# Column sums of the adaLN modulation rows: four TensorE transposes and a VectorE sum in place of four one-column products

## The chip, the cores and the metric

The kernel runs on one core of a Trainium2 chip. The metric is the device time of one execution in microseconds. A core has a matrix engine (TensorE, PE in the rows; its weight loads are listed apart as PEld), a vector engine (VectorE, DVE), a scalar engine (ScalarE, ACT), GpSimd (POOL) and a queue engine (SyncE, SP) that here issues the transfers from device memory. Products land in PSUM, in banks of 128 partitions by 512 fp32 columns.

## The reference

Two decoder layers over 256 tokens of width 1024. Each layer takes six vectors of 1024 numbers (shift, scale and gate for each of two halves) from the conditioning vector `c`:

```python
for l in range(DEPTH):
    mod = jax.nn.silu(c) @ ada_w[l] + ada_b[l]                 # (1, 6144)
    sh1, sc1, g1, sh2, sc2, g2 = jnp.split(mod[:, None, :], 6, axis=-1)
    h = rms_norm(x, norm_mix[l]) * (1.0 + sc1) + sh1
    x = x + g1 * token_mixing(h, ...)                          # three attention-like mixers, gates, w_out
    h = rms_norm(x, norm_ffn[l]) * (1.0 + sc2) + sh2
    f = swiglu(h, ...) if l % 2 == 0 else moe_ffn(h, ...)      # dense, then top-2 of 8 experts
    x = x + g2 * f
return rms_norm(x, final_norm)
```

All weights are fp32. `mod` is computed from `c` and `ada_w` alone, 2 x 6144 sums of 1024 products.

## The kernel before, in words

**Weights.** SP loads each weight as chunks of 1 MB (128 x 2048 fp32) into six buffers `raw`. ScalarE rounds a chunk to `w_hi` (line 1435) and VectorE computes the rest `w_lo` (line 1852), so that TensorE can build an fp32 product from three products of rounded parts (`mm3`, lines 743 to 745). In the first 970 us of the profile this goes in halves of a chunk with four slots (`HL`), and the engines split three halves ahead of TensorE (`AHEAD`). The expert stage after that uses whole chunks (`wide_hi`, `wide_lo`).

**Order.** The order of the work is written out by hand. The token-mixing stage of each layer follows the string `SLOTS`: before each piece of a large product stand the small steps of the mixers, among them `d` (a pair of modulation products) and `s` (its column sum); `KEPT` says which of them a layer keeps, six in layer 0 and four in layer 1. In the dense stage of layer 0 the class `Due` says after which chunks a pair and a sum come. Every engine runs through the same list, so each engine has its own queue in that order.

**Modulation.** The 12288 columns come in 24 blocks of 512. For a block, `ada_pair` multiplies the two chunks of `ada_w` (kept in fp32) with `silu(c)`. The 1024 rows are eight groups of 128; group k of a chunk goes to the quarter k of the partitions (32 partitions that all hold the same number), so a 128 x 512 bank `pO` then holds four partial rows, each 32 times. ScalarE copies it to the tile `acc` (`ada_copy`). Then the partial rows must be added and turned so that 512 columns become 128 partitions by 4 numbers of `mod`. Two functions do this: `ada_sum` writes a bank of `pT` and serves the `s` steps and the dense stage; `ada_sum_early` writes a bank of `pO` and serves the places around the norms. In both, four products use a 128 x 128 piece of `acc` as the stationary operand and the tile `quads` as the moving one. `quads` is one column that is 1 in the first partition of each quarter and 0 elsewhere, made once by VectorE from the identity matrix (line 2210).

VectorE then adds the bias and writes `mod` (`ada_columns`, line 1868, and `ada_columns_early`, line 1875). `mod` is used by `modulate` (line 1996 writes `hf`, the modulated rows), by `gate_row` (which spreads a gate over a bank) and, for the experts, at line 2426.

**Transposes.** Other parts of the kernel turn 128 x 128 fp32 blocks with TensorE transposes against the identity, four to a bank of `pT`, in the helper `turned` (line 801). Small products go through the helper `mm` (line 748).

**Waits.** `link` lets VectorE wait for the completion of its own last instruction before the next one issues. `take_T` and `take_O` make TensorE wait until the bank used two takes ago has been read; `free` is the semaphore that says so.

The functions that the diff touches and what calls them, with the line numbers of the profile:

Of the kernel before, what the change touches and what calls it, by code (L numbers as in the profile page):

```python
# [27 lines left out]
ALU = mybir.AluOpType  # L28
# [3 lines left out]
P = 128  # L32
# [313 lines left out]
def build(nc, a, table, out):  # L346
    ctx = ExitStack()
    with ctx:
        def sem(name):
            return ctx.enter_context(nc.semaphore(name))  # L350
# [41 lines left out]
        rope_t = sb("rope_t", [P, 8, HD])  # L392
        tmp = sb("tmp", [P, W])

        quads = sb("quads", [P, 1])
        acc = sb("acc", [P, W], at=(here[0] + 31) // 32 * 32)
        oT_hi[0] = sb("oTn_hi", [P, 4, SEQ], F32R)
        oT_lo[0] = sb("oTn_lo", [P, 4, SEQ], F32R)
# [105 lines left out]
        cols_ready = sem("cols_ready")  # L504
        csilu_ready = sem("csilu_ready")
        ada_used = sem("ada_used")
        quads_ready = sem("quads_ready")
        dve_link = sem("dve_link")
        act_link = sem("act_link")
        pool_link = sem("pool_link")  # L510
# [211 lines left out]
        def _(pe):  # L722
# [24 lines left out]
            def mm(dst, lhsT, rhs, first=True, last=True):  # L747
                return nc.tensor.matmul(dst, lhsT, rhs, start=first, stop=last, skip_group_check=True)  # L748
# [107 lines left out]
            def ada_sum():  # L856

                pe.wait_ge(O_free[b.O.slot(partials[0])], b.O.before(partials[0]) + 1)
                pt = take_T()
                for k in range(4):  # L860
                    ins = mm(pt[:, k:k + 1], acc[:, k * P:(k + 1) * P], quads[:, 0:1])
                ins.then_inc(T_full, 1)

            def ada_sum_early():

                pe.wait_ge(O_free[b.O.slot(partials[0])], b.O.before(partials[0]) + 1)
                po = take_O()
                for k in range(4):
                    ins = mm(po[:, k:k + 1], acc[:, k * P:(k + 1) * P], quads[:, 0:1])
                ins.then_inc(O_full, 1)  # L870

            pe.wait_ge(csilu_ready, 1)
            pe.wait_ge(quads_ready, 1)
            for j in range(EARLY):
                for _ in range(2):
                    b.adas.append(b.raw.take())
# [955 lines left out]
        def _(dve):  # L1832
# [24 lines left out]
            def ada_ended(first):  # L1857

                for what, n in due.after(first, b.hl.n // 2):
                    if what == "pair":  # L1860
                        skip(b.O, 1)
                    else:
                        ada_columns(n // ADA, n % ADA * 4, 1)

            def ada_columns(l, at, n):

                pt, free = T_in()
                V.tensor_tensor(mod[:, l, bass.ds(at, 4 * n)], pt[:, 0:4 * n], cols[:, l, bass.ds(at + R_ADAB, 4 * n)], ALU.add).then_inc(free, 1)

            def ada_columns_early(n):  # L1870

                l, at = n // ADA, n % ADA * 4
                skip(b.O, 1)
                po, free = O_in()
                V.tensor_tensor(mod[:, l, at:at + 4], po[:, 0:4], cols[:, l, at + R_ADAB:at + R_ADAB + 4], ALU.add).then_inc(free, 1)

            def ada_scale(l, at, w, n=8):

# [328 lines left out]
            link(V.memset(sq[:, :, :], 0.0))  # L2207
            dve.wait_ge(tab_in, 16)
            dve.wait_ge(cols_ready, DEPTH)
            V.tensor_reduce(quads[:, :], ident.rearrange("p (k n) -> p k n", k=CK)[:, :, 0], AX_X, ALU.add).then_inc(quads_ready, 1)  # L2210
            dve.wait_ge(x_in, 16)
            skip(b.raw, 2 * EARLY)
            for l in range(DEPTH):
# [31 lines left out]
                for subs, kind, which, i in MIXES[l]:  # L2245
                    for sub, c in subs:
                        if sub in ("k0", "kw", "kl", "k2", "k3"):
                            compression(sub, l)
                        elif sub in ("f0", "f1"):
                            forget_gates(sub, l)  # L2250
                        elif sub in ("a2", "a3"):
                            scores(sub, c, l)
                        elif sub[0] == "b" and o_uses(sub, c):
                            values(sub, c, l)
                        elif sub in ("a1", "a1b", "b1", "b2"):
                            skip(b.T, t_uses(sub, c))
                        elif sub == "o":
                            for q in range(2):
                                pt, free = T_in()
                                dve.wait_ge(oT_hi_ready, 6 * l + 2 * c + q + 1)  # L2260
                                V.tensor_tensor(oT_lo[c][:, 2 * q:2 * q + 2, :], pt[:, :].rearrange("p (k n) -> p k n", k=2),
                                                oT_hi[c][:, 2 * q:2 * q + 2, :].bitcast(F32), ALU.subtract).then_inc(oT_ready, 1)
                                dve.drain().then_inc(free, 1)
                        elif sub == "d":
                            skip(b.O, 1)
                        elif sub == "m":
                            lo_merged(0, 2)
                        elif sub == "s":
                            ada_columns(n_pair // ADA, n_pair % ADA * 4, 1)
                            n_pair += 1  # L2270
                    if last:
                        ended(*last, l)
                        if last == ("r", (2, 0), 1):
                            dve.drain().then_inc(merged_ready, 1)
                    split_to(b.hl.n + 1 + AHEAD)
                    b.hl.take()
                    last = (kind, which, i)
# [330 lines left out]
```

## Time and profile before

| | us |
|---|---|
| median of three runs | 2006.43 |
| lowest, highest | 2006.08, 2016.94 |
| profiled execution, first to last instruction (span) | 2005.2 |
| TensorE busy in it | 1933.1 (96%) |
| VectorE busy | 1473.8 (73%) |
| ScalarE busy | 1157.9 (58%) |

For the profiled execution only the span is listed; its own time is the span and about 1.2 us around it, if it lies as the median of the runs does (2006.43 - 2005.2). Busy time of TensorE has to be read with care: its matmuls overlap, the duration of one reaches into the next, and the distance from the start of one to the start of the next says what it costs. A matmul of fp32 operands is recorded twice (two passes), a transpose once.

```profile
PE   5999999999999999998999999999999999999996
PEclk9999999999999999999899999999999999999998
DMA  9745434585556644354799999999999999999993
```

These three lines cut the span into 40 slices of 50 us and give tenths: busy TensorE, the clock that it was granted, and the busy share of the 16 DMA engines. The modulation work lies in the first 20 slices, the experts in the other 20.

### The profile page before, as it was taken

The numbers are of one execution on the slowest core, as the hardware profiler recorded it, in microseconds if no ns is written. First come the engines' busy times: TensorE is split into PE (matmuls) and PEld (weight loads), VectorE is DVE, ScalarE is ACT, GpSimd is POOL, SyncE is SP. The second block draws the span as 40 slices with busy tenths as digits, with TensorE's granted clock in tenths as the row PEclk, the third lists the DMA queues.
The fourth block names the chain that finished last, engine by engine and source line by source line (L and its number), as shares of the span: only waits on it lengthen the run. The fifth ranks groups of instructions, "written<-read, shape, count | busy, mean of one in ns | idle before, by whom it ended". The sixth has DMA issues, their size and how long they took to land.

```text
span 2005.2 us, 27891 instructions
## 1 busy us (share of the span) xinstructions
PE 1933.1 (96%) x9976; PEld 1572.7 (78%) x9976; DVE 1473.8 (73%) x1504; ACT 1157.9 (58%) x1245; POOL 92.4 (5%) x134
## 2 busy tenths in 40 slices
PE   5999999999999999998999999999999999999996
PEld 2777888789987788887787787887878878778885
DVE  2755575744566655666788888889888888888988
ACT  1554554334434545543567767767677676766773
POOL 0510100000004300000000000000000000000000
PEclk9999999999999999999899999999999999999998
DMA  9745434585556644354799999999999999999993
GB/s 325 254 168 209 170 126 168 189 315 189 189 188 211 222 155 152 106 174 141 273 358 335 340 345 356 343 343 343 337 354 351 336 341 351 348 352 330 351 359 134
DMA packets 275630, 532.97 MB, mean 266 GB/s; under 512 B 10768, under 2 KB 23392, under 8 KB 275424
## 3 DMA queue, kind: packets, MB, share of 16 engines
q1 hardware_dynamic: 275552, 531.91, 75.6%
q8 instruction: 52, 0.85, 0.2%
q14 instruction: 26, 0.21, 0.0%
HBM read 530.83 MB, written 1.05 MB: 265 GB/s over the span
## 4 chain that ended last, share of the span: by engine, by line
PE 90%; DVE 5%; ACT 2%; issue 1%; DVEq 1%; DMA 0%; SPq 0%; ACTq 0%
PE pA L743 18%; PE pA L744 17%; PE pA L745 17%; PE pA L748 9%; PE pO L748 7%; PE pO L743 6%; PE pO L745 6%; PE pO L744 6%; PE pT L801 4%; DVE w_lo L1852 1%; PE pT L748 1%; ACT w_hi L1435 1%; DVE win L2085 0%; DMA x<-in_x 0%; PE pT L743 0%
## 5 line engine op out<-in xcount | busy, mean ns | idle before, releaser
L1893 DVE TENSOR_TENSOR wide_lo<-raw,wide_hi 128x2048 fp32r<-128x2048 f32 x336 | 762.5, 2290 | 123.2 <-ACT wide_hi L1435 103.6
L1435 ACT ACTIVATE wide_hi<-raw 128x2048 fp32r<-128x2048 f32 x336 | 644.7, 1921 | 214.6 <-PE pO L745 119.9
L1435 ACT ACTIVATE w_hi<-raw 128x1024 fp32r<-128x1024 f32 (+1 forms) x242 | 251.3, 1045 | 341.2 <-PE pA L745 249.8
L1852 DVE TENSOR_TENSOR w_lo<-raw,w_hi 128x1024 fp32r<-128x1024 f32 (+1 forms) x242 | 294.5, 1230 | 168.7 <-ACT w_hi L1435 159.7
L743 PE MATMUL pA<-wide_hi,x_lo 128*128 128x512 f32 x896 | 359.7, 401 | 1.4 <-DVE x_lo L2435 0.6
L745 PE MATMUL pA<-wide_hi,x_hi 128*128 128x512 f32 x896 | 355.0, 396 | 0.0
L744 PE MATMUL pA<-wide_lo,x_hi 128*128 128x512 f32 x896 | 354.9, 396 | 0.0
L743 PE MATMUL pA<-w_hi,h_lo 128*128 128x512 f32 (+2 forms) x560 | 227.4, 406 | 14.8 <-DVE w_lo L1852 10.9
L745 PE MATMUL pA<-w_hi,h_hi 128*128 128x512 f32 (+2 forms) x560 | 217.9, 389 | 0.0
L744 PE MATMUL pA<-w_lo,h_hi 128*128 128x512 f32 (+2 forms) x560 | 217.8, 389 | 0.0
L743 PEld LDWEIGHTS pA<-wide_hi,x_lo 128*128 128x128 f32 x896 | 168.7, 188 | 44.4 <-issue 3.8
L745 PEld LDWEIGHTS pA<-wide_hi,x_hi 128*128 128x128 f32 x896 | 168.5, 188 | 40.5
L744 PEld LDWEIGHTS pA<-wide_lo,x_hi 128*128 128x128 f32 x896 | 168.7, 188 | 38.1
L743 PE MATMUL pO<-wide_hi,aT_lo 128*128 128x512 f32 x448 | 180.1, 402 | 1.2 <-DVE aT_lo L2450 1.2
L745 PE MATMUL pO<-wide_hi,aT_hi 128*128 128x512 f32 x448 | 177.2, 396 | 0.0
L744 PE MATMUL pO<-wide_lo,aT_hi 128*128 128x512 f32 x448 | 176.9, 395 | 0.0
L743 PEld LDWEIGHTS pA<-w_hi,h_lo 128*128 128x128 f32 x560 | 107.7, 192 | 49.9 <-issue 22.3
L745 PEld LDWEIGHTS pA<-w_hi,h_hi 128*128 128x128 f32 x560 | 107.5, 192 | 23.2
L744 PEld LDWEIGHTS pA<-w_lo,h_hi 128*128 128x128 f32 x560 | 107.8, 193 | 19.3
L743 PEld LDWEIGHTS pO<-wide_hi,aT_lo 128*128 128x128 f32 x448 | 84.1, 188 | 21.7 <-issue 1.5
L745 PEld LDWEIGHTS pO<-wide_hi,aT_hi 128*128 128x128 f32 x448 | 84.2, 188 | 20.5
L744 PEld LDWEIGHTS pO<-wide_lo,aT_hi 128*128 128x128 f32 x448 | 84.3, 188 | 20.0
(273 smaller groups left out, 2391.1 us busy)
## 6 DMA issues: line engine op xcount, KB each, us to landing
raw<-in_moe_w SPq DMA_DIRECT2D x336, 1024.0 KB, 6.8
raw<-in_w_in SPq DMA_DIRECT2D x56, 1024.0 KB, 5.5
raw<-in_ada_w SPq DMA_DIRECT2D x48, 1024.0 KB, 6.6
raw<-in_ffn_w SPq DMA_DIRECT2D x33, 1024.0 KB, 5.2
raw<-in_w_out SPq DMA_DIRECT2D x8, 1024.0 KB, 5.0
raw<-in_cmp_k_w SPq DMA_DIRECT2D x4, 1024.0 KB, 5.9
raw<-in_cmp_v_w SPq DMA_DIRECT2D x4, 1024.0 KB, 10.6
raw<-in_w_read_nsa SPq DMA_DIRECT2D x4, 1024.0 KB, 6.1
```

Source lines behind the costliest of these rows:

```text
L743: nc.tensor.matmul(dst, xl, wh, start=first, stop=False, skip_group_check=True)
L744: nc.tensor.matmul(dst, xh, wl, start=False, stop=False, skip_group_check=True)
L745: return nc.tensor.matmul(dst, xh, wh, start=False, stop=last, skip_group_check=True)
L748: return nc.tensor.matmul(dst, lhsT, rhs, start=first, stop=last, skip_group_check=True)
L801: ins = nc.tensor.transpose(pt[0:m, i * width:i * width + n], src, ident[0:n, 0:n])
L1435: return nc.scalar.activation(dst, src, ACT.Copy)
L1852: V.tensor_tensor(w_lo[m][:, 0:n], raw[s][:, i * n:(i + 1) * n], w_hi[m][:, 0:n].bitcast(F32), ALU.subtract).then_inc(raw_done, 1)
L1893: V.tensor_tensor(wide_lo[m][:, :], raw[g][:, :], wide_hi[m][:, :].bitcast(F32), ALU.subtract).then_inc(raw_done, 2)
```

## The change

The four products with `quads` become four transposes of the same 128 x 128 pieces of `acc`, each into its own 128 columns of the bank. The column p of a transposed piece holds partition p of `acc`, so the four partial rows stand in columns 0, 32, 64 and 96 of each piece. VectorE sums them: one reduction reads 4 x 4 elements per partition, 32 columns apart, from PSUM and writes 4 numbers to `mod`; it waits for its own result (`link`), adds the bias in place and only then frees the bank. `quads`, its semaphore and the wait for it are gone, and the tiles allocated behind it move down by 32 bytes.

```diff
-        quads = sb("quads", [P, 1])
...
-                    ins = mm(pt[:, k:k + 1], acc[:, k * P:(k + 1) * P], quads[:, 0:1])
+                    ins = nc.tensor.transpose(pt[:, k * P:(k + 1) * P], acc[:, k * P:(k + 1) * P], ident)
                 ins.then_inc(T_full, 1)
...
-                    ins = mm(po[:, k:k + 1], acc[:, k * P:(k + 1) * P], quads[:, 0:1])
+                    ins = nc.tensor.transpose(po[:, k * P:(k + 1) * P], acc[:, k * P:(k + 1) * P], ident)
                 ins.then_inc(O_full, 1)
...
-            pe.wait_ge(quads_ready, 1)
...
+            def column_sums(l, at, pt, free):
+
+                link(V.tensor_reduce(mod[:, l, at:at + 4], pt[:, :].rearrange("p (j q n) -> p j q n", j=4, q=CK)[:, :, :, 0], AX_X, ALU.add))
+                V.tensor_tensor(mod[:, l, at:at + 4], mod[:, l, at:at + 4], cols[:, l, at + R_ADAB:at + R_ADAB + 4], ALU.add).then_inc(free, 1)
+
+            def ada_columns(n):
 
                 pt, free = T_in()
-                V.tensor_tensor(mod[:, l, bass.ds(at, 4 * n)], pt[:, 0:4 * n], cols[:, l, bass.ds(at + R_ADAB, 4 * n)], ALU.add).then_inc(free, 1)
+                column_sums(n // ADA, n % ADA * 4, pt, free)
 
             def ada_columns_early(n):
 
-                l, at = n // ADA, n % ADA * 4
                 skip(b.O, 1)
                 po, free = O_in()
-                V.tensor_tensor(mod[:, l, at:at + 4], po[:, 0:4], cols[:, l, at + R_ADAB:at + R_ADAB + 4], ALU.add).then_inc(free, 1)
+                column_sums(n // ADA, n % ADA * 4, po, free)
...
-            V.tensor_reduce(quads[:, :], ident.rearrange("p (k n) -> p k n", k=CK)[:, :, 0], AX_X, ALU.add).then_inc(quads_ready, 1)
```

## Rows read from the trace of the kernel before

**Rows 1.** Busy time by stretch: us, engines with counts, PEclk, DMA share, GB/s.

```profile
11.00:970.00 959.00, 915.62 (x5399) 753.31 (x5400) 569.69 (x841) 435.86 (x692) 91.96 (x129) 0.97 0.57 194
970.00:1985.00 1015.00, 1012.97 (x4565) 816.82 (x4566) 888.20 (x634) 716.74 (x547) 0.00 (x0) 1.00 0.95 340
```

**Rows 2.** Waits of TensorE from 0 to 985 us: total us, times, longest.

```profile
PE pA L743 <- DVE w_lo L1852: 11.9, 7, 4.6
...
PE pO L748 <- ACT acc L1435: 4.1, 1, 4.1
```

**Rows 3.** The one-column products: duration ns min/median/max, first and last start, forms.

```profile
L748 PE MATMUL pT<-quads,acc x112: 164/250/271, 68.7 to 781.2; 128*128 128x1 f32 x112
...
L748 PE MATMUL pO<-quads,acc x80: 169/250/375, 19.7 to 958.3; 128*128 128x1 f32 x80
```

**Rows 4.** Timeline of TensorE, one group between large products: start us, us, instruction.

```profile
68.69 0.95 PE L748 MATMUL pT<-quads,acc 128*128 128x1 f32 x8
69.50 0.48 PE L743 MATMUL pA<-w_hi,h_lo 128*128 128x512 f32 x1
```

**Rows 5.** Timeline of TensorE, four existing transposes between large products.

```profile
295.37 0.60 PE L801 MATMUL pT<-tab,S 128*128 128x128 f32 x4
295.72 0.48 PE L743 MATMUL pA<-w_hi,oTr_lo 128*128 128x512 f32 x1
```

**Rows 6.** Timeline of TensorE at the half clock, transposes and then a group.

```profile
598.30 1.97 PE L801 MATMUL pT<-tab,y 128*128 128x128 f32 x8 [2.98 <-DVE y L1986]
...
600.06 1.71 PE L748 MATMUL pO<-quads,acc 128*128 128x1 f32 x8
...
601.70 3.50 PE L748 MATMUL pO<-raw,csilu 128*32 128x512 f32 x16
```

**Rows 7.** Timeline of VectorE, a linked reduction out of PSUM and its successor.

```profile
957.78 0.17 DVE L2401 TENSOR_REDUCE rs<-pA 128x1 f32<-128x8 f32 x1 [1.38 <-PE pA L748]
957.98 0.17 DVE L2402 TENSOR_TENSOR rs<-pA,rs 128x16 f32<-128x16 f32 x1
```

**Rows 8.** Groups by line and shape, VectorE: busy us, mean ns, idle before.

```profile
L2045 DVE TENSOR_REDUCE stat<-S 128x8 f32<-128x120 f32 x4 | 1.1, 278 | 0.1
```

**Rows 9.** Waits of VectorE from 0 to 985 us.

```profile
DVE w_lo L1852 <- ACT w_hi L1435: 159.7, 102, 6.0
```

**Rows 10.** Timeline, TensorE group or transposes and the VectorE instruction that reads them.

```profile
25.83 0.95 PE L748 MATMUL pO<-quads,acc 128*128 128x1 f32 x8
...
26.82 0.16 DVE L1875 TENSOR_TENSOR mod<-pO,cols 128x4 f32<-128x4 f32 x1 [5.04 <-PE pO L748]
...
392.45 0.60 PE L801 MATMUL pT<-tab,y 128*128 128x128 f32 x4
...
393.09 0.99 DVE L1996 TENSOR_SCALAR hf<-pT,mod 128x256 f32<-128x256 f32 x2 [0.63 <-PE pT L801]
```

**Rows 11.** Timeline, the last sum of the dense stage.

```profile
437.42 1.05 PE L748 MATMUL pT<-quads,acc 128*128 128x1 f32 x8 [0.72 <-ACT acc L1435]
...
437.92 0.69 DVE L2330 TENSOR_TENSOR aTd_lo<-a_T,aTd_hi 128x512 fp32r<-128x512 f32 x1 [2.27 <-ACT aTd_hi L1435]
438.52 0.15 DVE L1868 TENSOR_TENSOR mod<-pT,cols 128x4 f32<-128x4 f32 x1
```

**Rows 12.** Timeline of TensorE, the waits behind the last two sums.

```profile
944.35 1.85 PE L748 MATMUL pA<-routw,hf 128*128 128x8 f32 x8 [1.53 <-DVE hf L1996]
...
960.80 6.66 PE L748 MATMUL pA<-sel,y 128*128 128x128 f32 x32 [2.24 <-DVE mod L1875]
```

**Rows 13.** Busy time by stretch, columns as in rows 1: clock at three places.

```profile
741.50:744.90 3.40, 3.40 (x9) 2.65 (x8) 2.69 (x7) 0.00 (x0) 0.00 (x0) 0.50 0.46 175
180.00:186.00 6.00, 6.00 (x36) 4.78 (x33) 4.97 (x7) 3.65 (x11) 0.00 (x0) 1.00 0.02 7
...
216.80:217.60 0.80, 0.80 (x9) 0.78 (x8) 0.00 (x0) 0.52 (x1) 0.00 (x0) 1.00 1.06 402
```

**Rows 14.** Groups by line and shape, TensorE transposes: busy us, mean ns, idle before.

```profile
L801 PE MATMUL pT<-tab,S 128*128 128x128 f32 x144 | 20.1, 275 | 0.0
```

More of the change, by code:

```diff
@@ L506, in build @@
         ada_used = sem("ada_used")
-        quads_ready = sem("quads_ready")
         dve_link = sem("dve_link")
@@ L1862, in ada_ended @@
                     else:
-                        ada_columns(n // ADA, n % ADA * 4, 1)
-            def ada_columns(l, at, n):
+                        ada_columns(n)
+            def column_sums(l, at, pt, free):
+                link(V.tensor_reduce(mod[:, l, at:at + 4], pt[:, :].rearrange("p (j q n) -> p j q n", j=4, q=CK)[:, :, :, 0], AX_X, ALU.add))
+                V.tensor_tensor(mod[:, l, at:at + 4], mod[:, l, at:at + 4], cols[:, l, at + R_ADAB:at + R_ADAB + 4], ALU.add).then_inc(free, 1)
+            def ada_columns(n):
                 pt, free = T_in()
-                V.tensor_tensor(mod[:, l, bass.ds(at, 4 * n)], pt[:, 0:4 * n], cols[:, l, bass.ds(at + R_ADAB, 4 * n)], ALU.add).then_inc(free, 1)
+                column_sums(n // ADA, n % ADA * 4, pt, free)
             def ada_columns_early(n):
-                l, at = n // ADA, n % ADA * 4
                 skip(b.O, 1)
                 po, free = O_in()
-                V.tensor_tensor(mod[:, l, at:at + 4], po[:, 0:4], cols[:, l, at + R_ADAB:at + R_ADAB + 4], ALU.add).then_inc(free, 1)
+                column_sums(n // ADA, n % ADA * 4, po, free)
             def ada_scale(l, at, w, n=8):
@@ L2268, in _ @@
                         elif sub == "s":
-                            ada_columns(n_pair // ADA, n_pair % ADA * 4, 1)
+                            ada_columns(n_pair)
                             n_pair += 1
```

## The prediction

> **What bounds the kernel now.** I read the busy time by stretch first. Between 11 and 970 us, where all modulation work lies, TensorE is busy for 915.62 of 959 us while VectorE is busy for 569.69, ScalarE for 435.86, and the DMA share is 0.57; after 970 us it is busy for 1012.97 of 1015 us [rows 1]. So TensorE bounds both parts, and the second part has none of the changed work: it only starts earlier or later. Next come the waits of TensorE in the first part. They are few and short, the largest sum being 11.9 us for `w_lo`, and on the changed path the largest is 4.1 us, for the copy to `acc` ahead of the first sum [rows 2]. What the reader is to see: outside such waits, a microsecond taken off TensorE's queue is a microsecond off the end, and one added to VectorE mostly is not.
>
> **How many.** The one-column matmuls are recorded 112 times into `pT` and 80 times into `pO` [rows 3]. A sum has four of them, each recorded twice, so there are 192 / 8 = 24 sums, 14 and 10.
>
> **TensorE, per sum.** Durations mislead here, since they overlap: start-to-start distances count. A group of one-column products between two large products takes 69.50 - 68.69 = 0.81 us [rows 4]. Four existing fp32 transposes in the same surroundings take 295.72 - 295.37 = 0.35 us [rows 5]; the product behind shows the same 0.48 us in both, so nothing is hidden in it. The old group costs four matmuls in two passes with a weight load each, the transpose one pass. The saving is 0.46 us; I take 0.45, because at some places a group is followed by something other than a large product.
>
> The Trainium skill, TensorE: Matmul & The Clock Gate, in its section on why a gap is 56 ns, puts the start-to-start floor of a tiny matmul near 25 ns and that of 128 columns at 55.6 ns. By it alone eight one-column passes (0.20 us) would cost no more than four transposes (0.22 us), and the sum of this document would be nought. The row shows 0.81 us, four times that, so the matmul floor is not what paces the group here.
>
> **Where it counts.** Of the 24 sums, 19 stand in TensorE's queue with other TensorE work right behind them and no wait that ends elsewhere: 19 x 0.45 = 8.55 us. The other five:
> - At 25.83 us, and in the same form once more behind the same norm, the sum heads a chain through `mod`, `hf` and the first split to a TensorE wait. What counts is the time to VectorE's next instruction: 26.82 - 25.83 = 0.99 us before; four transposes are read after 393.09 - 392.45 = 0.64 us [rows 10]. The gain of 0.35 us less the VectorE term below (0.20) is 0.15 us each, 0.3 together.
> - At 437.42 us `mod` is held by VectorE's `aTd_lo`, which starts at 437.92, takes 0.69 us and comes from ScalarE, not by the sum [rows 11]: no gain, and VectorE's 0.20 us is added.
> - Behind the last sum but one TensorE waits 1.53 us for `hf` [rows 12], which VectorE makes ahead of this `mod`: no gain, no loss.
> - Behind the last one it waits 2.24 us until VectorE has read the bank [rows 12]. VectorE comes to it late, after the router's chain, so nothing is gained and 0.20 us is added.
>
> **The half clock.** At 600.06 us the clock is low, and the group takes 601.70 - 600.06 = 1.64 us against (600.06 - 598.30) / 2 = 0.88 us for four transposes [rows 6]. That would save 0.76 us, but what follows then runs at the low clock for longer; I keep 0.45 and leave the rest to the range. The first sum is alike.
>
> **VectorE, per sum.** Added is one reduction (16 elements read from PSUM, 4 written) with a wait for itself. The nearest row is a linked reduction of 8 elements out of PSUM: its successor starts 957.98 - 957.78 = 0.20 us after it [rows 7]. That is the lower bound too. The upper bound is the reduction of 120 elements, 0.278 us [rows 8], with the 0.03 us that the wait leaves in rows 7 between end and start: 0.31. I take 0.20, since rows 7 have the same form and nearly the size. In all 24 x 0.20 = 4.8 us of VectorE. Queued behind it are mostly the next `w_lo` subtraction or `hf`. VectorE itself waits 159.7 us, 102 times, for ScalarE's `w_hi` in this part [rows 9], and the splits run three halves ahead, so this cover absorbs it; without the cover all 4.8 us would come back. Where the halves restart behind a norm (once in the dense stage of layer 0, once in the mixing of layer 1; both are among the seven waits for `w_lo` or their like in rows 2) VectorE's chain may be tight; I charge 0.1 us each, half a reduction.
>
> **Banks.** A bank of `pT` or `pO` is freed 0.20 us later after a read that starts up to 0.35 us earlier. Nil. ScalarE's copy, SP's queue and the transfers are unchanged: no DMA is added or moved, and the buffers of `ada_w` are released by `ada_pair`, not by the sum. POOL is not touched. The removed wait for `quads` and its one reduction lie in front of TensorE's first load of `ada_w`, which ends later: nil. The tiles move by 32 bytes: nil.
>
> **Sum.** -8.55 - 0.3 + 0.2 + 0.2 + 0.2 = -8.25 us. Against the profiled execution this is 2005.2 - 8.25 = 1996.95 us of span; the median of the runs stands 1.2 us above the span, so I predict 1998.2 us, 0.4% less.
>
> **Rival 1: nothing is left of it.** Either the transpose of `acc` paces like the products did (for instance because it is recorded in two passes after all, which would be the change not doing what it says), or the shorter queue turns into waits for `w_lo`. Against it: four transposes of this shape have four records [rows 5]. For it: every late VectorE term counted would return 4.8 us. Time: 2006.43 - 8.25 + 4.8 = 2003.0 if only VectorE's time returns, 2006.4 if the pace is as before, 2011 with both. Chance 0.14.
>
> **Rival 2: slower, by the clock.** The clock is granted for stretches of time, and the same token-mixing sequence ran at 1.00 in layer 0 (180 to 186 us) but at 0.50, the 1.2 GHz level, for 3.4 us in layer 1 (741.5 to 744.9 us) [rows 13]. Such a stretch costs at most half of itself, 1.7 us. Transposes in place of products, in the ten sums that `KEPT` leaves to the mixing stages and the nine others inside dense stretches, might let the clock fall behind each of them. The gain of 8.25 us is used up at five added stretches; with one behind each of the 19 it is 19 x 1.7 - 8.25 = +24.1, 2030.5 us. Against it: eight transposes in a row at 216.8 us ran at 1.00 with 1.00 behind [rows 13]. Chance 0.05, of which 0.03 beyond 1%.
> The Trainium skill, same page, section on PE-mode transpose, says that the full clock "doesn't engage for transpose-mode". By that rule this rival would be the rule and not the exception. The row at 216.8 us does not agree with it.
>
> **Rival 3: by the durations.** If the recorded durations were the cost, a sum would fall from 8 x 0.25 = 2.0 us [rows 3] to 4 x 0.275 = 1.1 us [rows 14]: 24 x 0.9 = 21.6 us, 1984.8 us. Against it: the start-to-start distances of the groups above. Chance 0.02.
>
> **How the numbers follow.** The forecast has 0.79. Its own range: down to 24 x 0.46 + 2 x 0.3 for the low-clock sums + 1.7 x 2 if two of the low stretches go, 2006.43 - 15 = 1991.4; up to the gain with VectorE at 0.31 on ten of its sums and one added stretch, 2006.43 - 8.25 + 3.1 + 1.7 = 2003. The range 1992 to 2006 adds the greater part of rival 1. A measurement of this kernel can tell a change of about 1% from none, and the whole gain is 0.4%: faster by over 1% is below 1986.4 us, which only rival 3 reaches; slower by over 1% is above 2026.5, which only rival 2 reaches.
>
> **What would show it.** In the profile after: 24 x 4 transposes of `acc` at one record each; 0.35 us from the start of a group to the next product (at 0.8 the first step is wrong); `mod` reductions near 0.17 us with the sum behind them 0.20 us later; TensorE's wait for `w_lo` in total no more than 1 us above 11.9; the wait before the gather near 2.24 + 0.45 + 0.20 = 2.9 us; the expert stage starting about 8 us earlier and of the same length. A clock below 0.97 in the first part would speak for rival 2. The prediction is wrong if the end moves by less than 3 us although the groups shrink as said.

## The result and the profile after

| | us, median of 6 | lowest to highest | profiled span |
|---|---|---|---|
| before | 2006.51 | 2006.04 to 2019.20 | 2005.2 |
| after | 1995.86 | 1995.13 to 1997.09 | 1993.3 |

The ratio is 0.9923, with a 95% interval from 0.9897 to 0.9950. The change takes 10.65 us off; forecast were 8.25, to 1998.2 us. Direction and order of size came out as said, and the time lies in the range. The forecast itself lies just outside the interval, whose smallest gain is 10.0 us. (The ratio also counts the two runs of the kernel before that took 2016.94 and 2019.20 us, so it shows more than the medians do.) The run that was profiled took 1995.13 us, 1.8 us above its span and not 1.2, which doesn't touch the gain. So something worth about 2.4 us was missing, and the experiments look for it.

Busy time by stretch of the kernel after, the columns as in rows 1:

```profile
11.00:960.00 949.00, 903.64 (x5304) 737.59 (x5305) 573.67 (x866) 436.18 (x692) 92.05 (x129) 0.98 0.57 196
960.00:1975.00 1015.00, 1011.32 (x4567) 814.76 (x4565) 889.64 (x635) 717.42 (x550) 0.00 (x0) 1.00 0.95 340
```

Against [rows 1] TensorE is still busy for nearly all of both parts (95% and 99.6%). The first part has shrunk by ten microseconds, the second is as it was; the first expert product starts at 959.47 us instead of 969.82. All but 1.6 of the 11.9 us between the two profiled spans were won ahead of the experts.

The transposes of `acc` by tile, kernel after (duration in ns min/median/max, first and last start in us):

```profile
L859 PE MATMUL pT<-tab,acc x56: 271/273/328, 68.0 to 773.7; 128*128 128x128 f32 x56
...
L867 PE MATMUL pO<-tab,acc x40: 272/273/473, 20.1 to 947.9; 128*128 128x128 f32 x40
```

56 + 40 = 96 = 24 x 4: one record each, where [rows 3] had eight records for a sum. Timeline of TensorE, kernel after, at the place of [rows 4]:

```profile
67.98 0.60 PE L859 MATMUL pT<-tab,acc 128*128 128x128 f32 x4
68.33 0.48 PE L741 MATMUL pA<-w_hi,h_lo 128*128 128x512 f32 x1
```

From group to product it is 0.35 us instead of 0.81, as the existing transposes had shown [rows 5]. VectorE at the same place:

```profile
68.62 0.17 DVE L1864 TENSOR_REDUCE mod<-pT 128x4 f32<-128x16 f32 x1 [0.92 <-PE pT L859]
68.83 0.16 DVE L1865 TENSOR_TENSOR mod<-mod,cols 128x4 f32<-128x4 f32 x1
```

The reduction takes 0.17 us and the sum starts 0.21 us behind it, as [rows 7]. Waits of TensorE and then of VectorE, kernel after, from 0 to 985 us (in total, times, longest), against [rows 2, 9]:

```profile
PE pA L741 <- DVE w_lo L1849: 12.2, 8, 4.8
...
PE pO L867 <- ACT acc L1432: 4.2, 1, 4.2
...
PE pA L746 <- DVE mod L1865: 2.3, 1, 2.3
...
PE pT L746 <- DVE mod L1865: 1.5, 1, 1.5
```

```profile
DVE w_lo L1849 <- ACT w_hi L1432: 160.0, 101, 6.8
```

TensorE waits 0.3 us more for `w_lo` in all: VectorE's added 5 us are absorbed. The wait for `mod` ahead of the gather is 2.3 us, where 2.9 had been forecast. The one for `hf` ahead of the router's first product has grown from 1.53 to 1.88 us: from the group to that product it is 2.48 us in both kernels, so nothing is won there, as forecast.

One more view, the clock. Timeline of TensorE, kernel after, at the place of [rows 6], and behind it three stretches of the same kernel, the columns as in rows 1. The first two hold the work that the kernel before does about 5.6 and 7.5 us later, from 741.5 and 813 us on:

```profile
595.15 1.97 PE L799 MATMUL pT<-tab,y 128*128 128x128 f32 x8 [3.01 <-DVE y L1987]
596.91 1.06 PE L867 MATMUL pO<-tab,acc 128*128 128x128 f32 x4
597.90 3.55 PE L746 MATMUL pO<-raw,csilu 128*32 128x512 f32 x16
```

```profile
735.90:739.30 3.40, 3.40 (x19) 2.80 (x18) 2.73 (x8) 0.62 (x1) 0.00 (x0) 1.00 0.39 148
805.40:809.40 4.00, 4.00 (x19) 3.31 (x18) 3.90 (x6) 1.51 (x3) 0.00 (x0) 1.00 0.00 0
...
181.70:188.50 6.80, 6.80 (x21) 5.23 (x20) 3.11 (x9) 0.83 (x1) 0.00 (x0) 0.52 0.00 0
```

At the low clock the group behind the norm at the start of layer 1 takes 0.99 us instead of 1.64. The work that ran at 0.50 from 741.5 us [rows 13] runs at 1.00 now, and so does that of the stretch at 813 us, which before stood at 0.57 (its row is below). In exchange 6.8 us from 181.7 us are at 0.52, and the same work (185.5 to 192.3 us there) stood at 1.00 before. The low stretches have moved, and they have become fewer.

What stands ahead of the two stretches is of use later. Timeline of TensorE, first the kernel before at 739 us, then the kernel after at the same work:

```profile
739.23 1.99 PE L748 MATMUL pO<-vc,PT 15*128 15x64 f32 x16
741.15 0.56 PE L743 MATMUL pA<-w_hi,h_lo 128*128 128x512 f32 x1
```

```profile
733.67 1.99 PE L746 MATMUL pO<-vc,PT 15*128 15x64 f32 x16
735.59 0.50 PE L741 MATMUL pA<-w_hi,h_lo 128*128 128x512 f32 x1
```

The change touches neither instruction. Small products of the mixers stand right ahead of the low stretch, and the nearest one-column group of the kernel before starts at 728.67 us, 12 us earlier. The low stretch at 181.7 us of the kernel after stands behind the same products in layer 0.

**A measure for the clock.** Every run comes with its span and its mean granted clock. The granted level is 1.00 or 0.50 of 2.4 GHz, so 2 x (1 - mean clock) x span is the time spent at the low level; I call it low-clock time. Over all runs of this study, taken within each kernel, the span grows by 0.44 us with each us of it (a least-squares slope over 193 runs). This gives a second number per kernel, the corrected span = mean span - 0.44 x low-clock time, in which instructions and waits are left and the clock is not. It is an estimate worked out from the runs. Its standard error is at most 1 us for each kernel (single runs scatter by 0.7 to 2.3 us), and the mean clock is listed to 0.001, so the low-clock time of one run comes in steps of 4 us. The kernel before has runs near 2018 us among its usual 2007 (22 of 80 over the whole study), with 89.3 us of low-clock time against 66.6, which is why means and medians differ here, and why a comparison with its mean and one with its usual runs give two numbers.

### The profile page after: what moved, and what is told of

It reads as the page before. It is cut to its first block, busy times and chain, and to the rows that moved or that the text cites. A ratio compares the mean times of both kernels' runs of the same rounds, so it can differ in the third digit from the quotient of the medians.

```text
span 1993.3 us, 27723 instructions
## 1 busy us (share of the span) xinstructions
PE 1919.3 (96%) x9880; PEld 1555.2 (78%) x9880; DVE 1476.8 (74%) x1527; ACT 1157.7 (58%) x1245; POOL 92.5 (5%) x134
## 3 DMA queue, kind: packets, MB, share of 16 engines
HBM read 530.83 MB, written 1.05 MB: 267 GB/s over the span
## 4 chain that ended last, share of the span: by engine, by line
PE 89%; DVE 6%; ACT 2%; issue 1%; DMA 1%; DVEq 1%; SPq 0%; ACTq 0%
PE pA L741 18%; PE pA L743 17%; PE pA L742 17%; PE pA L746 8%; PE pO L746 7%; PE pO L741 6%; PE pO L743 6%; PE pO L742 6%; PE pT L799 4%; DVE w_lo L1849 1%; ACT w_hi L1432 1%; DMA raw<-in_ffn_w 1%; PE pT L746 0%; DMA x<-in_x 0%; DVE win L2086 0%
## 5 line engine op out<-in xcount | busy, mean ns | idle before, releaser
L746 PE MATMUL pA<-h_hi,w_lo 128*128 128x256 f32 x352 | 99.0, 281 | 0.6 <-DVE w_lo L1849 0.6
```

## The experiments

All kernels in one table; "products" counts the groups of one-column products in each, and a set is a group of four transposes of `acc`.

| kernel | runs | median us | products | low-clock us | corrected span |
|---|---|---|---|---|---|
| before | 80 | 2007.2 | 24 | 72.9 | 1976.0 |
| after | 6 | 1995.9 | 0 | 59.8 | 1967.8 |
| e1_pe_twice (24 sets more) | 10 | 2005.6 | 0 | 59.3 | 1976.2 |
| e2_dve_twice | 9 | 1996.8 | 0 | 60.3 | 1969.6 |
| e3_before_shift1 | 10 | 2007.6 | 24 | 63.0 | 1978.0 |
| e4_before_shift2 | 10 | 2010.2 | 24 | 69.1 | 1979.3 |
| e5_after_shift1 | 10 | 1995.5 | 0 | 55.8 | 1969.8 |
| e6_after_shift2 | 10 | 1999.2 | 0 | 60.7 | 1971.0 |
| e7_before_twice | 4 | 2044.9 | 48 | 105.2 | 1995.7 |
| e8_late_only | 10 | 2002.8 | 10 | 68.9 | 1971.2 |
| e9_pe_three (48 sets more) | 10 | 2012.2 | 0 | 56.7 | 1985.6 |
| e10_plus_products | 10 | 2019.5 | 24 | 69.0 | 1986.7 |
| e11_early_only | 10 | 2008.4 | 14 | 71.8 | 1973.5 |
| e12_fill | 4 | 1987.4 | 0 | 37.7 | 1969.1 |

Already the first two lines split the result: 1976.0 - 1967.8 = 8.2 us of work in the queue, and 13.1 us less low-clock time, which at 0.44 is 5.7 us between the means. Against the usual 2007-us runs alone (66.6 us, corrected span 1975.5) it is 7.7 us of work and 6.8 x 0.44 = 3.0 us of clock. The two parts of such a split add up to the difference of the mean spans by construction; what is measured is how it divides. At 0.50 us for each us, which is all that half the clock can cost work that TensorE bounds, the first split would be 7.4 and 6.5 us.

### e1_pe_twice

The changed kernel with each of its groups of transposes issued twice.

```diff
-                for k in range(4):
+                for k in [*range(4)] * 2:
```

> The changed kernel with the four transposes of each of the 24 sums issued twice (the second four overwrite the first). Theory Q (the gain is TensorE queue time): four transposes cost about 0.38 us of queue where nothing else waits, 19 sums in the queue and 2 in chains: 21 x 0.38 = 8.0 us more than the changed kernel, 1995.9 + 8.0 = 2003.9 us, give or take 3 us for half-clock stretches that move. Rival C (the extra 2.4 us over my sum are half-clock stretches that happened to vanish): same sum, but time from start of a group to the next product still 0.35 + 0.38 us, and the mean granted clock tells the rest: time less half of the low-clock time lines up. Rival S (each sum saves more than 0.45 us, about 0.56): the group costs little, so the added four give less than 6 us.

Measured: ratio to before 0.9971 [0.9948, 0.9995]. Against after, the corrected span grows by 8.4 us for 24 more sets, 0.35 us each. The low-clock time is unchanged, 59.3 against 59.8. So a set costs what the start-to-start distance says, not the 1.1 us of its durations, and no effect of more transposes on the clock is seen (the standard errors of the two means are 2 to 3 us).

### e2_dve_twice

VectorE's linked reduction twice, TensorE untouched.

```diff
-                link(V.tensor_reduce(mod[:, l, at:at + 4], ..., AX_X, ALU.add))
+                for _ in range(2):
+                    link(V.tensor_reduce(mod[:, l, at:at + 4], ..., AX_X, ALU.add))
```

> The changed kernel with the linked reduction of each sum done twice by VectorE. My sum: 0.20 us each, of which only the two chains behind norms, the last sum of the dense stage and the last sum of all stand on the path, with 0.1 us at two restarts: 1.0 us more, 1996.9 us. Rival D (VectorE is not covered by its waits for ScalarE): all 24 x 0.20 = 4.8 us come back, 2000.7 us. Give or take 1.5 us for each half-clock stretch of 3.4 us that comes or goes.

Measured: ratio 0.9931 [0.9907, 0.9955], corrected span 1.8 us above after, give or take 0.7. 24 reductions of 0.20 us are 4.8 us of VectorE; under half of it shows. The cover is real. Whether it is thinner than the 1.0 us that the forecast's terms for VectorE come to (four of 0.20 and two of 0.10) this run can't tell.

### e3_before_shift1, e4_before_shift2, e5_after_shift1, e6_after_shift2

Each delays the queue once, early, by spare transposes ahead of the first sum of `ada_sum`: 16 in shift1, 32 in shift2, in the kernel before and after. They ask whether the clock depends on where the work falls.

```diff
+                if not shifted:
+                    shifted.append(1)
+                    for k in [*range(4)] * 4:
+                        nc.tensor.transpose(pt[:, k * P:(k + 1) * P], acc[:, k * P:(k + 1) * P], ident)
```

> The kernel before with 16 spare transposes of acc in front of the products of the first sum of the token-mixing stage (at about 68 us), nothing else changed: TensorE's queue gets 16 x 0.095 = 1.5 us longer once and everything behind it is late by that. Queue theory with fixed half-clock stretches: 2006.5 + 1.5 = 2008.0 us and the mean clock of before, 0.983. Rival C (which stretches run at half clock depends on where the work falls in time): stretches near 741 and 813 us vanish or others appear, 1.5 us each; the time is off 2008.0 by multiples of 1.5 us and the mean clock differs from 0.983.

> As the run with 16 spare transposes, with 32: 3.0 us longer once at about 68 us. Fixed stretches: 2009.5 us at mean clock 0.983. Rival C: another set of half-clock stretches than the kernel before and than the one with 16 spare transposes, the time off 2009.5 by multiples of 1.5 us, downward if the stretches near 741 and 813 us go.

> The changed kernel with 16 spare transposes of acc in front of the first sum of the token-mixing stage: 1.5 us more of TensorE queue once. What the runs so far show: within a kernel the span follows the low-clock time (twice the missing mean clock times the span) with 0.46 us per us; with that taken off, the changed kernel is 7.7 us under the kernel before, near my 8.25. Theory C (the 2.4 us beyond my sum are low-clock time that depends on where work falls in time, not on transposes): corrected span 1.5 us (up to 2.4, as the shifted kernel before had) above the changed kernel; low-clock time anywhere from 50 to 75 us, so the median from 1993 to 2003. Rival T (transposes in place of one-column products keep the clock up by themselves): low-clock time stays at the changed kernel's 60 us or below, median 1997.5.

> As before with 32 spare transposes, 3.0 us once. Theory C: corrected span 3.0 to 3.6 us above the changed kernel, low-clock time another again, 50 to 75 us. Rival T: low-clock time 60 us or below, median 1999.

Measured: corrected spans 2.0 and 3.3 us above before, 2.0 and 3.2 above after, where 1.5 and 3.0 us of transposes were added. The times move otherwise: the kernel before with 16 transposes more takes 2007.6 us, 0.4 above its own median, since its low-clock time is 63.0 us where the usual runs without the delay have 66.6. The mean of all runs without it is 72.9; the rest of that difference is that none of the ten runs with the delay fell near 2018 us. With 32 the mean is 69.1. After stays near its own: 59.8, 55.8, 60.7. In the profiles with a delay the low stretches away from the norms stand at other places in part: the ones near 741 and 813 us are there with 16 transposes more, only the second with 32. A delay that changes no other work can so shift the low-clock time by some 4 us, or 1.6 us of the end, in the usual runs, and by 10 us in the mean. Part of what one pair shows can be placement.

### e7_before_twice

The opposite of e1: the kernel before with its one-column products doubled.

```diff
-                for k in range(4):
+                for k in [*range(4)] * 2:
                     ins = mm(pt[:, k:k + 1], acc[:, k * P:(k + 1) * P], quads[:, 0:1])
```

> The kernel before with the four one-column products of each of the 24 sums issued twice. Theory Q: a group costs 0.81 to 0.88 us of queue: 19 in the queue and 2 in chains give 21 x 0.85 = 17.9 us more than before in the corrected span, 2025 us in the median give or take 3. Rival (the floor of a tiny matmul, about 25 ns each, paces a group and not its weight loads): 21 x 0.2 = 4.2 us more, 2011 us. Rival T: low-clock time grows above the 73 us mean of before, since one-column products leave the array idle.

Measured: ratio 1.0170 [1.0127, 1.0214], +37.7 us between the medians. Corrected, the span is 19.7 us longer (24 groups, 0.82 us each), which is the 0.81 us of [rows 4] once more; the 0.2 us a group of the rival would have given a quarter. Timeline of TensorE in this kernel:

```profile
72.53 1.84 PE L748 MATMUL pT<-quads,acc 128*128 128x1 f32 x16
74.23 0.48 PE L743 MATMUL pA<-w_hi,h_lo 128*128 128x512 f32 x1
```

1.70 us for two groups, 0.85 each. The rest is the clock: 105.2 us low against 72.9, 32.3 x 0.44 = 14.2 us of the 34.0 us between the mean spans. Busy time of this kernel by stretch, the first part and then three short ones:

```profile
11.00:960.00 949.00, 912.55 (x5336) 752.00 (x5337) 536.61 (x766) 423.72 (x678) 89.27 (x128) 0.96 0.55 186
141.00:147.50 6.50, 6.50 (x31) 5.50 (x30) 4.63 (x6) 1.66 (x2) 4.37 (x5) 0.69 1.05 392
181.70:188.50 6.80, 6.80 (x39) 6.12 (x39) 2.74 (x5) 1.44 (x2) 0.00 (x0) 0.70 1.05 392
216.00:222.00 6.00, 6.00 (x37) 5.71 (x37) 4.26 (x10) 0.61 (x4) 0.00 (x0) 0.71 0.17 60
```

and the kernel before, behind its row at 813 us, in the three stretches that hold the same work as the short ones above, 3 to 14 us earlier there:

```profile
813.00:817.00 4.00, 4.00 (x12) 3.10 (x12) 3.90 (x6) 0.16 (x1) 0.00 (x0) 0.57 0.00 0
```

```profile
137.90:144.40 6.50, 6.50 (x36) 4.91 (x35) 4.54 (x7) 2.64 (x3) 5.25 (x5) 1.00 1.04 391
172.10:178.90 6.80, 6.80 (x46) 5.92 (x46) 3.06 (x6) 2.49 (x3) 0.00 (x0) 1.00 1.05 394
202.40:208.40 6.00, 6.00 (x41) 5.25 (x40) 5.29 (x11) 0.90 (x5) 0.00 (x0) 1.00 0.17 65
```

With doubled products the clock falls in the midst of stretches in which TensorE has no recorded idle time (6.50 of 6.50 us busy); with the single group it stands at 1.00 at the same work. In this profile six of the low stretches, from 143.4, 170.7, 184.4, 218.5, 764.6 and 819.3 us, begin during a doubled group of the mixing stages or at most 1.2 us behind it; the other three of those stages, at 123, 710 and 778 us, do not. In the kernel before none of the low stretches of the mixing stages (116.8, 741.4, 813.1 us) begins at such a group.

### e8_late_only and e11_early_only

The change for one kind of sum alone: the 14 of `ada_sum` (`pT`) in e8, the 10 of `ada_sum_early` (`pO`) in e11, the rest as before. The diff of e8; that of e11 is the same with `po`:

```diff
-                    ins = mm(pt[:, k:k + 1], acc[:, k * P:(k + 1) * P], quads[:, 0:1])
+                    ins = nc.tensor.transpose(pt[:, k * P:(k + 1) * P], acc[:, k * P:(k + 1) * P], ident)
...
-                V.tensor_tensor(mod[:, l, bass.ds(at, 4 * n)], pt[:, 0:4 * n], ...).then_inc(free, 1)
+                link(V.tensor_reduce(mod[:, l, at:at + 4], pt[:, :].rearrange(...)[:, :, :, 0], AX_X, ALU.add))
+                V.tensor_tensor(mod[:, l, at:at + 4], mod[:, l, at:at + 4], ...).then_inc(free, 1)
```

> Only the 14 sums that go through a pT bank use transposes and the VectorE sum; the 10 around the norms keep the one-column products. By my sum 13 of the 14 stand in TensorE's queue: 13 x 0.45 less 0.2 for the last of the dense stage = 5.65 us less than before in the corrected span; rival D (VectorE's reduction not covered): 14 x 0.2 less of a gain, 3.1 us. The median follows the low-clock time, 1997 to 2005 us.

> Only the 10 sums around the norms, through pO banks, use transposes and the VectorE sum. Six of them stand in TensorE's queue: 6 x 0.45 + 0.3 for two chains - 0.2 behind the last - 0.2 for two restarts = 2.6 us less than before in the corrected span. Rival D: 10 x 0.2 less, 1.0 us. Together with the complementary run the two should add up to the whole change, 7.7 to 8.2 us. Low-clock time between that of before (73) and of the changed kernel (60).

Measured: corrected, 4.7 us and 2.5 us below before, together 7.2 of the 8.2 us of the whole. The parts add up, within their spread. The low-clock times, 68.9 and 71.8 us, stay at the level of the kernels with products; neither half alone shows the gain of the clock. Each interval ([0.9953, 0.9993] and [0.9942, 0.9992]) shows a gain, but it counts the runs of before near 2018 us, and e11's median of 2008.4 us is above the 2007.2 of before. The medians, 2002.8 and 2008.4 us, don't rank the halves either: their clocks differ.

### e9_pe_three

The rival to "the products cost the clock" was "any lengthening of the small work does". Three sets of transposes per sum lengthen a group by as much as doubled products do.

```diff
-                for k in range(4):
+                for k in [*range(4)] * 3:
```

> The changed kernel with the four transposes of each of the 24 sums issued three times. Two extra sets cost 2 x 8.5 us by the run with one extra set: 17 us more corrected span than the changed kernel, about as much queue as the kernel before gained from doubled one-column products. Theory P (one-column products leave the array so little to do that the clock falls; with them doubled the low-clock time was 105 us, with them as before 73, without them 60): low-clock time stays at 60 us give or take 7, median 1995.9 + 17 = 2013. Rival L (a longer piece of any small work in front of the large products has the same effect): low-clock time near 100 us, median near 2031.

Measured: ratio 1.0008 [0.9984, 1.0032]; corrected span +17.8 us over after, 0.37 us a set. The low-clock time is 56.7 us, the second lowest among the kernels that only add or swap work, against 105.2 in e7 with nearly the same added time. Its transposes by tile and its first part by stretch:

```profile
L859 PE MATMUL pT<-tab,acc x168: 270/273/327, 72.5 to 794.8; 128*128 128x128 f32 x168
```

```profile
11.00:960.00 949.00, 907.91 (x5397) 746.28 (x5397) 561.02 (x827) 431.82 (x686) 92.06 (x129) 0.98 0.56 191
```

The clock of the first part is 0.98 with 288 transposes of `acc` in it, 0.96 in e7. So the low-clock time of e7 does not come from the length of the added work but from its kind.

### e10_plus_products

The changed kernel with the old products issued ahead of the transposes, into the same bank; the transposes overwrite them.

```diff
+                for k in range(4):
+                    mm(pt[:, k:k + 1], acc[:, k * P:(k + 1) * P], quads[:, 0:1])
                 for k in range(4):
                     ins = nc.tensor.transpose(pt[:, k * P:(k + 1) * P], acc[:, k * P:(k + 1) * P], ident)
```

> The changed kernel with the four one-column products put back in front of the four transposes of each sum, into the same bank, their result overwritten. Corrected span 21 x 0.85 = 17.9 us (20.4 by the run with doubled products) above the changed kernel. Theory P: low-clock time rises to that of the kernel before or above it, 73 to 90 us, median 2020 to 2028. Rival L': low-clock time as in the run with tripled transposes, whatever that is, since the length of the added work is alike.

Measured: ratio 1.0043 [1.0021, 1.0065]; corrected span 18.9 us above after, 0.79 us a group; low-clock time 69.0 us against 59.8. Putting the products back brings back most of the low-clock time (9.2 of 13.1 us). Against e9, the same kernel with nearly the same time added as transposes, it is 69.0 to 56.7 us.

### e12_fill

If low-clock time has a price it can be attacked by itself. This is the changed kernel with bf16 products of zeros where TensorE would wait, into banks that are free at that point: ten ahead of each of two early pieces of layer 0's first `w` product and at the start of layer 1, six ahead of the transposes of `y` behind the second norm of each layer, and six each ahead of the router and of the gather.

```diff
+            def fill(dst, n):
+                for _ in range(n):
+                    mm(dst[:, :].rearrange("p (k n) -> p k n", k=CK), zeros[:, :], zeros[:, :].unsqueeze(1).broadcast_to([P, CK, P]))
...
+                    if l == 0 and i in (0, 2):
+                        pe.wait_ge(pool_link, 1)
+                        fill(pA[2], 10)
...
+                    fill(pA[2], 10)
...
+                evacuated(b.T, T_free, 2)
+                fill(pT[b.T.slot(b.T.n)], 6)
...
+                    fill(dst, 6)
...
+                    fill(pA[1], 6)
```

> The changed kernel with idle TensorE time in front of known waits filled by matmuls of a zero tile (512 columns, bf16) into banks that the next product overwrites: 10 each at the two first waits for w_lo and at the start of layer 1, 6 each behind the two other norms, in front of the router's products and in front of the gather. If idle time is what brings the clock down at these places, low-clock time falls by 7 to 20 us and the median by 3 to 9 us, to 1987 to 1993. Rival Z (zeros in the array do not hold the clock, or the fill is in the way): low-clock time stays at 60 us and the median is 1996 or, where the fill outlasts the wait, up to 2002.

Measured: 1987.4 us, ratio 0.9883 [0.9839, 0.9928], 19.8 us below before and 8.5 below after. The corrected span is 1969.1 us against 1967.8, 1.3 us more with a standard error of 1.2, so the fillers cost nearly nothing; the low-clock time is 37.7 us against 59.8, and 22.1 x 0.44 = 9.7 us. Its fillers by tile, and two stretches by busy time:

```profile
L746 PE MATMUL pA<-zeros x42: 379/379/634, 26.3 to 942.6; 128*128 128x512 bf16 x42
...
L746 PE MATMUL pT<-zeros x12: 379/379/390, 376.9 to 924.5; 128*128 128x512 bf16 x12
```

```profile
11.00:960.00 949.00, 914.69 (x5402) 742.13 (x5403) 581.03 (x870) 444.50 (x697) 92.18 (x129) 0.99 0.58 197
584.00:594.00 10.00, 9.25 (x62) 4.26 (x61) 8.22 (x21) 1.82 (x4) 0.00 (x0) 1.00 0.71 228
```

The same work in the kernel after, 6 us later there, where the norm leaves TensorE idle for 3 us:

```profile
590.00:600.00 10.00, 6.99 (x42) 3.44 (x44) 8.22 (x21) 1.40 (x4) 0.00 (x0) 0.72 0.60 210
```

With most of the idle time filled the start of layer 1 runs at 1.00 instead of 0.72. Its four runs (1984.7 to 1990.4 us) all beat every run of both kernels.

## Where the prediction was right, and the step that failed

- **24 sums, 0.81 to 0.35 us in the queue.** Right: 0.35 us in the timeline after. e1 and e9 price a set at 0.35 and 0.37, e7 and e10 a group of products at 0.82 and 0.79; the difference is 0.42 to 0.47 where I took 0.45.
- **The sum of -8.25 us.** Right as a sum of instructions, within about a microsecond: the corrected spans differ by 8.2 us, or by 7.7 against the usual runs of before. The part by function, 4.7 and 2.5 us, is as expected within a microsecond.
- **VectorE covered.** Right in the main: the wait for `w_lo` grew by 0.3 us, and e2 returns 1.8 of 4.8 us, 0.7 either way.
- **The last sum, gather wait 2.9 us.** Wrong in size: 2.3. VectorE at this place, kernel after:

```profile
949.39 0.48 DVE L2416 TENSOR_SCALAR sel<-tab,slot 128x128 f32<-128x128 f32 x2 [1.14 <-issue]
949.78 0.17 DVE L1864 TENSOR_REDUCE mod<-pO 128x4 f32<-128x16 f32 x1
949.99 0.16 DVE L1865 TENSOR_TENSOR mod<-mod,cols 128x4 f32<-128x4 f32 x1
```

  and TensorE:

```profile
947.21 1.09 PE L867 MATMUL pO<-tab,acc 128*128 128x128 f32 x4
950.59 6.50 PE L746 MATMUL pA<-sel,y 128*128 128x128 f32 x32 [2.29 <-DVE mod L1865]
```

  VectorE comes to the sum late, as forecast, and pays its 0.21 us. From the start of the group to the gather it is 3.38 us, and was 960.80 - 957.53 = 3.27: 0.11 us more, where I had charged 0.20. The 0.45 us that I added to the wait was a slip in the reading: idle time is counted from the recorded end of the group, and counted from the start of the group that end came no earlier. The four transposes last 1.09 us by the record, since the clock stands at 0.50 over them; the eight products lasted 1.03 us at 1.00. So this group lost by the clock what it had gained by the transposes.
- **The last sum of the dense stage.** I had "no gain, and VectorE's 0.20 us is added" [rows 11]. TensorE and VectorE at this place, kernel after, and ScalarE behind them:

```profile
433.89 0.66 PE L859 MATMUL pT<-tab,acc 128*128 128x128 f32 x4 [0.72 <-ACT acc L1432]
436.01 0.68 PE L746 MATMUL pT<-tab,mod 128*128 128x128 f32 x4 [1.46 <-DVE mod L1865]
```

```profile
433.39 0.69 DVE L2322 TENSOR_TENSOR a_T<-a_T,pA 128x512 f32<-128x512 f32 x1
434.77 0.69 DVE L2330 TENSOR_TENSOR aTd_lo<-a_T,aTd_hi 128x512 fp32r<-128x512 f32 x1 [0.70 <-ACT aTd_hi L1432]
435.38 0.17 DVE L1864 TENSOR_REDUCE mod<-pT 128x4 f32<-128x16 f32 x1
```

```profile
434.11 0.63 ACT L1432 ACTIVATE aTd_hi<-a_T 128x512 fp32r<-128x512 f32 x1 [0.28 <-DVE a_T L2322]
```

  From the group to `gate_row`'s transposes it is 436.01 - 433.89 = 2.12 us; before it was 438.94 - 437.42 = 1.52. So 0.60 are added, not 0.20: besides VectorE's 0.21, `aTd_lo` starts 0.88 us behind the group instead of 0.50. It needs ScalarE's `aTd_hi`, which now waits 0.28 us for VectorE's `a_T`; before it did not wait, for `a_T` had started at 434.96, 2.46 us ahead of the group, and now starts 0.50 us ahead of it. The group comes 3.53 us earlier than before, VectorE's `a_T` only 1.57. A group that comes earlier in front of a chain that is held elsewhere only waits longer.
- **The half clock, costed at nought: the failed term.** I wrote "I keep 0.45 and leave the rest to the range". The sum of -8.25 us has no term for the clock. The argument has it as rival 2, on the slower side, and on the faster side only in the lower end of the range ("1.7 x 2 if two of the low stretches go"). In its place the runs showed a term of about -3 us. Low-clock time fell from 66.6 us in the usual runs of the kernel before to 59.8, at 0.44 us per us, which is 3.0 us; with the 7.7 us of work that is 10.7 against the measured 10.65. Against the mean of all runs of before (72.9) it is 5.7 us. That the end of the range allowed for two low stretches that go, and that two of layer 1 went, was luck in so far as nothing in the forecast says why they should.
- **What causes it.** The six kernels without one-column products and without fillers (after, e1, e2, e5, e6, e9) have 55.8 to 60.7 us, those with them 63.0 to 105.2. Doubling them adds 32.3 us, putting them back adds 9.2, and lengthening by transposes adds nothing. That added one-column products cost clock is shown, most clearly where they are doubled. That those 24 groups cost the kernel before its 6.8 us (13.1 in the mean) is not shown, and the cause in this pair stays open. Taking out the products of either kind of sum alone moved little (e8, e11), a bare shift moved the usual runs of before by 3.6 us (e3) and the kernel after by 4.0 at most, and the two low stretches of layer 1 that went stood behind small products of the mixers and not behind a one-column group. The same products `vc,PT` are followed by 0.50 in layer 1 of the kernel before and by 1.00 in layer 1 of the kernel after, and the other way round in layer 0. Placement is a rival that no run here rules out. What in a one-column product lowers the clock was not tried.
- **Rival 1**, nothing left, fell with e1 and with the 0.35 us. **Rival 3**, by the durations, fell with e1: 8.4 us for 24 sets, not 26. **Rival 2**, slower by the clock, fell plainly: 24 and 48 added sets left the low-clock time at 59.3 and 56.7 us. Its sentence from the Trainium skill (TensorE: Matmul & The Clock Gate, the section on PE-mode transpose), that the full clock does not engage for transposes, doesn't hold for this kernel: twelve in a row stand in a stretch at 1.00 in e9 (its row is in the last section), and the first part of e9 is at 0.98 with 288 of them. The page's floor of 25 ns for a tiny matmul does not price these products either, which cost 0.10 us for each of eight passes.

## What to carry to other kernels

Price small matmuls by the distance from their start to the next instruction's, since the durations overlap; here that forecast 8.25 us, and 7.7 to 8.2 were measured. Then write the clock down as a term with a sign: mean granted clock and span of each run give the low-clock time, and each us of it cost 0.44 us. Where TensorE bounds a kernel and waits a few microseconds behind a norm or a router, products of zeros into a free bank can be worth as much as a change in the work itself (8.5 us here between the medians).

## What was unexpected of the hardware

- The granted clock can fall while TensorE is recorded as busy without a gap. At one place of layer 0, behind four transposes of `S`, e7 has eight one-column fp32 products recorded in 16 passes and e9 twelve fp32 transposes. Timeline of TensorE and busy time by stretch, first e7, then e9:

```profile
142.25 2.31 PE L748 MATMUL pT<-quads,acc 128*128 128x1 f32 x16
144.43 0.77 PE L743 MATMUL pA<-w_hi,h_lo 128*128 128x512 f32 x1
```

```profile
141.50:148.00 6.50, 6.50 (x31) 5.46 (x30) 4.14 (x6) 1.39 (x2) 3.87 (x5) 0.65 1.05 390
```

```profile
140.19 1.47 PE L859 MATMUL pT<-tab,acc 128*128 128x128 f32 x12
141.42 0.48 PE L741 MATMUL pA<-w_hi,h_lo 128*128 128x512 f32 x1
```

```profile
139.50:146.00 6.50, 6.50 (x39) 5.10 (x38) 4.07 (x8) 2.54 (x3) 4.76 (x5) 1.00 1.05 390
```

  TensorE is busy for 6.50 of 6.50 us in both and the DMA share is 1.05 in both; the clock is 0.65 in e7, where it falls 1.1 us behind the start of the group, and 1.00 in e9. The product behind the group lasts 0.77 us in the one and 0.48 in the other.
- A delay of 1.5 us at one early place hid most of its own cost: the median is 2007.6 us against 2007.2, since the low-clock time is 3.6 us under that of the usual runs of the kernel before.
